# Contiguous gate and up halves in the weight slot, and expert rows fetched four experts ahead

## The reference

```python
scores = sigmoid(x @ router_w)
_, idx = top_k(scores + router_bias, 8)
wsel = sel / sum(sel) * 2.5                       # sel: the scores at idx
gates = sum(one_hot(idx, 64) * wsel[..., None], axis=1)
hid = silu(einsum('nd,edf->nef', x, exp_w_gate)) * einsum('nd,edf->nef', x, exp_w_up)
routed = einsum('nef,efd->nd', hid * gates[..., None], exp_w_down)
shared = (silu(x @ shared_w_gate) * (x @ shared_w_up)) @ shared_w_down
y = rmsnorm(x0 + g_f * (routed + shared))
```

## Time and profile before

| | us |
|---|---|
| three runs, median | 993.21 |
| lowest, highest | 984.48, 999.41 |
| profiled execution, first to last instruction (span) | 998.1 |
| TensorE busy in it | 798.7 (80%) |
| mean busy share of the 16 DMA engines, 350 to 955 us | 0.93 |

### The profile page before, as it was taken

The page is one execution under the profiler, slowest core; times in us unless marked ns, Lnnn a source line. Parts: engine busy times, 40 slices in busy tenths (PEclk is TensorE's granted clock), DMA queues, the critical chain, the costliest instruction groups (busy, mean ns, idle before and its releaser), DMA issues.

```text
span 998.1 us, 16529 instructions
## 1 busy us (share of the span) xinstructions
PE 798.7 (80%) x5564; PEld 449.7 (45%) x5565; DVE 393.9 (39%) x825; ACT 235.7 (24%) x405; POOL 306.1 (31%) x285
## 2 busy tenths in 40 slices
PE   1979999999888799876796888888788788887910
PEld 1657555445444355443443444444444344443500
DVE  2235183656144643233342343334334334444306
ACT  2112543023132222122121221222122122222202
POOL 0120000021133444344334343433334434344323
PEclk8879999999897889878888889887888988988965
DMA  9977846345689999989998999899899989999234
GB/s 273 398 244 240 304 164 231 117 149 212 226 251 362 367 318 334 324 251 348 311 316 287 315 316 327 252 349 310 281 340 321 360 285 334 358 331 353 68 58 145
DMA packets 192230, 277.75 MB, mean 278 GB/s; under 512 B 20355, under 2 KB 154931, under 8 KB 183548
## 3 DMA queue, kind: packets, MB, share of 16 engines
q1 hardware_dynamic: 165654, 250.88, 72.3%
q0 software_dynamic: 21216, 22.57, 10.2%
q10 hardware_dynamic: 5254, 2.76, 1.1%
HBM read 270.14 MB, written 25.89 MB: 297 GB/s over the span
## 4 chain that ended last, share of the span: by engine, by line
PE 54%; DMA 26%; issue 10%; DVE 6%; POOL 1%; POOLq 1%; ACT 1%; SPq 1%; DVEq 0%
DMA et<-xn_rows,idx 16%; PE bank L1049 15%; PE bank L1085 12%; DMA acc_rows<-et,idx 5%; PE bank L770 4%; PE bank L778 3%; PE bank L1032 3%; PE bank L913 3%; PE bank L797 2%; DMA gu<-in_ada_w 2%; PE bank L755 2%; DMA small<-halfc 2%; PE bank L1009 1%; PE bank L1136 1%; PE bank L781 1%
## 5 line engine op out<-in xcount | busy, mean ns | idle before, releaser
L1049 PE MATMUL bank<-gu,et 128*64 128x256 f32 x2496 | 295.9, 394 | 33.3 <-issue 31.0
L1049 PEld LDWEIGHTS bank<-gu,et 128*64 128x64 f32 x2496 | 185.6, 144 | 168.2 <-issue 91.4
L1085 PE MATMUL bank<-dn,et 128*64 128x512 f32 x624 | 183.5, 726 | 2.3 <-DVE et L1534 1.2
L449 POOL DMA_INDIRECT acc_rows<-et,idx x64 | 105.6, 1649 | 226.1 <-DVE et L1541 164.1
L430 POOL DMA_INDIRECT et<-xn_rows,idx x64 | 80.8, 1263 | 193.9 <-DVE idx L1516 133.7
L1534 DVE COPY et<-bank 128x256 f32<-128x256 f32 x64 | 27.1, 424 | 222.8 <-PE bank L1066 218.6
L690 ACT ACTIVATE et<-bank 64x512 f32<-64x512 f32 x64 | 37.8, 590 | 265.9 <-PE bank L1049 263.1
L1032 PE MATMUL bank<-ident,et 128*128 128x128 f32 x256 | 50.0, 328 | 62.3 <-DMA et<-xn_rows,idx 35.6
L1085 PEld LDWEIGHTS bank<-dn,et 128*64 128x64 f32 x624 | 46.6, 163 | 88.7 <-issue 88.7
L1520 DVE COPY et<-bank 128x512 f32<-128x512 f32 x64 | 44.3, 692 | 103.5 <-PE bank L1032 99.9
L1541 DVE TENSOR_SCALAR et<-bank,pick_out 128x512 f32<-128x512 f32 x64 | 48.1, 751 | 81.4 <-PE bank L1085 76.5
(11 more groups left out here) (269 smaller groups left out, 684.0 us busy)
## 6 DMA issues: line engine op xcount, KB each, us to landing
gu<-in_exp_w_gate SPq DMA_DIRECT2D x64, 1024.0 KB
gu<-in_exp_w_up SPq DMA_DIRECT2D x64, 1024.0 KB
dn<-in_exp_w_down SPq DMA_DIRECT2D x64, 1024.0 KB
gu<-in_ada_w SPq DMA_DIRECT2D x12, 2048.0 KB, 13.9
gu<-in_w_in SPq DMA_DIRECT2D x4, 2048.0 KB, 19.5
gu<-in_w_out SPq DMA_DIRECT2D x2, 2048.0 KB, 13.1
acc_rows<-dn SPq DMA_DIRECT2D x2, 1280.0 KB, 16.2
small<-halfc POOLq DMA_DIRECT2D x100, 0.0 KB
```

Source lines behind the costliest of these rows:

```text
L449: pool.indirect_dma_start(acc_rows[0], bass.IndirectOffsetOnAxis(ap=idx[:, u, 0:1], axis=0), yo[:, u % 2, 0, :], None, bounds_check=2 * T ...
L1049: mm = pe.matmul(bank[u % 2][64 * c:64 * c + 64, b * FE:(b + 1) * FE], xt[:, b, k % 4, k // 4, :], w[:, k, c * FE:(c + 1) * FE], start=(k ...
L1085: mm = pe.matmul(bank[5 + b][64 * c:64 * c + 64, :], hT[:, b, j, :], dn[:, dslot(u), j * D + c * HALF:j * D + (c + 1) * HALF], start=(j == ...
```

## The change

It does two things. First, a slot of `gu` is now seen as two halves of 8 KB per partition, [gate | up], so each gate and each up load (the shared expert's too) writes 8 KB in a row; the products read `w[:, c, k, :]` in place of `w[:, k, c*256:(c+1)*256]`. Second, G = 4: the gathers use four buffers (the two old ones, and the first two tiles of `xn`, which are free by then) and run four experts ahead, with four semaphores each for `gathered` and `gathered2`; select, pick and index move with them, from u+2 to u+4. Experts 2 and 3 are now picked and indexed before the loop.

```diff
+G = 4
+        xg_buf = [xg[:, 0], xg[:, 1]] + [xn[:, t, :].rearrange("p (s n) -> p s n", s=2) for t in range(2)]
...
-        eg = io["exp_w_gate"][0].rearrange("e (p k) f -> e p k f", k=KT)
+        eg = io["exp_w_gate"][0].rearrange("e (p k) f -> e p (k f)", k=KT)
...
+        def halves(slot):
+            return gu[slot][:, :, :].rearrange("p k n -> p (k n)").rearrange("p (c m) -> p c m", c=2)
+        def pair(slot):
+            return halves(slot).rearrange("p c (k f) -> p c k f", k=KT)
...
-                sync.dma_start(gu[gslot(u)][:, :, 0:FE], eg[e]).then_inc(ld_gu[gslot(u)], 16)
-                sync.dma_start(gu[gslot(u)][:, :, FE:2 * FE], eu[e]).then_inc(ld_gu[gslot(u)], 16)
+                sync.dma_start(halves(gslot(u))[:, 0, :], eg[e]).then_inc(ld_gu[gslot(u)], 16)
+                sync.dma_start(halves(gslot(u))[:, 1, :], eu[e]).then_inc(ld_gu[gslot(u)], 16)
...
+            pool.wait_ge(s["tp_ready"], TP["z11"] + 1)
...
-                if not (isinstance(e, int) and e < 2):
-                    pool.wait_ge(s["xt_ready"], e - 1)
+                if not (isinstance(e, int) and e < G):
+                    pool.wait_ge(s["xt_ready"], e - (G - 1))
...
-                    if not (last and u >= U - 2):
-                        gather(r, i + (u + 2) // U, (u + 2) % U)
+                    if not (last and u >= U - G):
+                        gather(r, i + (u + G) // U, (u + G) % U)
...
-                gather(r, 0, 0)
-                gather(r, 0, 1)
+                for u in range(G):
+                    gather(r, 0, u)
...
-                                           w[:, k, c * FE:(c + 1) * FE], start=(k == 0), stop=(k == KT - 1))
+                                           w[:, c, k, :], start=(k == 0), stop=(k == KT - 1))
...
-                    if not (last and u >= U - 2):
-                        pick(r, i + (u + 2) // U, (u + 2) % U)
+                    if not (last and u >= U - G):
+                        pick(r, i + (u + G) // U, (u + G) % U)
...
+                for u in range(2, G):
+                    pick(r, 0, u)
                 turn_x(r, 0, 0, is_full(r, 0, 0))
...
+                for u in range(2, G):
+                    select(r, 0, u)
+                    index(r, 0, u)
                 xt0(r, 0, 0)
```

More of the change, by code:

```diff
@@ L180, in build @@
         ld_shared_gu, ld_shared_dn = sem("ld_shared_gu"), sem("ld_shared_dn")
-        gathered = [sem("gathered0"), sem("gathered1")]
-        gathered2 = [sem("gathered2_0"), sem("gathered2_1")]
+        gathered = [sem(f"gathered{b}") for b in range(G)]
+        gathered2 = [sem(f"gathered2_{b}") for b in range(G)]
         scattered = [sem("scattered0"), sem("scattered1")]
@@ L190, in build @@
         wout_p = io["w_out"][0].rearrange("(k p) (j n) -> j p k n", p=P, n=512)
-        eg = io["exp_w_gate"][0].rearrange("e (p k) f -> e p k f", k=KT)
-        eu = io["exp_w_up"][0].rearrange("e (p k) f -> e p k f", k=KT)
+        eg = io["exp_w_gate"][0].rearrange("e (p k) f -> e p (k f)", k=KT)
+        eu = io["exp_w_up"][0].rearrange("e (p k) f -> e p (k f)", k=KT)
         ed = io["exp_w_down"][0].rearrange("e (p j) n -> e p (j n)", j=2)
@@ L296, in _ @@
             for c, name in enumerate(("shared_w_gate", "shared_w_up")):
-                sync.dma_start(gu[SH_SLOT][:, :, c * FE:(c + 1) * FE],
-                               io[name][0].rearrange("(p k) f -> p k f", k=KT)).then_inc(ld_shared_gu, 16)
+                sync.dma_start(halves(SH_SLOT)[:, c, :],
+                               io[name][0].rearrange("(p k) f -> p (k f)", k=KT)).then_inc(ld_shared_gu, 16)
             def load_gu(r, i, u):
@@ L426, in gather @@
                 pool.wait_ge(s["idx_ready"], e + 1)
-                if not (isinstance(e, int) and e < 2):
-                    pool.wait_ge(s["xt_ready"], e - 1)
+                if not (isinstance(e, int) and e < G):
+                    pool.wait_ge(s["xt_ready"], e - (G - 1))
                 pool.sem_inc(s["pool_go"], 1)
-                pool.indirect_dma_start(xg[:, u % 2, 0, :], None, xn_half,
+                pool.indirect_dma_start(xg_buf[u % G][:, 0, :], None, xn_half,
                                         bass.IndirectOffsetOnAxis(ap=idx[:, u, 0:1], axis=0),
-                                        bounds_check=2 * T - 1, oob_is_err=False).then_inc(gathered[u % 2], 16)
+                                        bounds_check=2 * T - 1, oob_is_err=False).then_inc(gathered[u % G], 16)
                 with pool.If(full):
-                    pool.indirect_dma_start(xg[:, u % 2, 1, :], None, xn_half,
+                    pool.indirect_dma_start(xg_buf[u % G][:, 1, :], None, xn_half,
                                             bass.IndirectOffsetOnAxis(ap=idx[:, u, 1:2], axis=0),
-                                            bounds_check=2 * T - 1, oob_is_err=False).then_inc(gathered2[u % 2], 16)
+                                            bounds_check=2 * T - 1, oob_is_err=False).then_inc(gathered2[u % G], 16)
                 with pool.Else():
-                    pool.dma_start(skipped[:, u:u + 1], halfc[0:1, :]).then_inc(gathered2[u % 2], 16)
+                    pool.dma_start(skipped[:, u:u + 1], halfc[0:1, :]).then_inc(gathered2[u % G], 16)
             def scatter(r, i, u):
@@ L945, in _, with shared_product @@
             wout(2, range(4, KT))
-            def shared_gu(t):
-                tile_product(bank[4 + t], t, gu[SH_SLOT], 2 * FE).then_inc(s["sh_ready"], 1)
+            def shared_product(t, ks):
+                t0, n = TILES[t]
+                w = pair(SH_SLOT)
+                for k in ks:
+                    if t < 2:
+                        mm = pe.matmul(bank[4 + t][:, :].rearrange("p (c f) -> p c f", c=2), xT[:, k, t0:t0 + n], w[:, :, k, :],
+                                       start=(k == 0), stop=(k == KT - 1))
+                    else:
+                        for c in range(2):
+                            mm = pe.matmul(bank[4 + t][64 * c:64 * c + 64, 0:FE], xT[:, k, t0:t0 + n], w[:, c, k, :],
+                                           start=(k == 0), stop=(k == KT - 1))
+                return mm
             def logits(t):
@@ L962, in _ @@
             pe.wait_ge(ld_shared_gu, 32)
-            tile_product(bank[4], 0, gu[SH_SLOT], 2 * FE, range(4))
+            shared_product(0, range(4))
             turn("z", "xn_ready", 1)
-            tile_product(bank[4], 0, gu[SH_SLOT], 2 * FE, range(4, KT)).then_inc(s["sh_ready"], 1)
+            shared_product(0, range(4, KT)).then_inc(s["sh_ready"], 1)
             pe.wait_ge(s["tp_evac"], TP["z11"] + 1)
@@ L981, in _ @@
             spread_gf(3)
-            tile_product(bank[5], 1, gu[SH_SLOT], 2 * FE, range(4))
+            shared_product(1, range(4))
             pe.wait_ge(s["mask_done"], 1)
@@ L995, in _ @@
             mm.then_inc(s["tp_ready"], 1)
-            tile_product(bank[5], 1, gu[SH_SLOT], 2 * FE, range(4, KT)).then_inc(s["sh_ready"], 1)
+            shared_product(1, range(4, KT)).then_inc(s["sh_ready"], 1)
             def pick(r, i, u):
@@ L1016, in turn_x @@
                 e = r * NE + i * U + u
-                pe.wait_ge(gathered[u % 2], 8 * (e - u % 2) + 16)
-                pe.wait_ge(gathered2[u % 2], 8 * (e - u % 2) + 16)
+                pe.wait_ge(gathered[u % G], (16 // G) * (e - u % G) + 16)
+                pe.wait_ge(gathered2[u % G], (16 // G) * (e - u % G) + 16)
                 if isinstance(e, int) and e == 0:
@@ L1027, in half @@
                     for k in range(4):
-                        pe.transpose(bank[2 + b][:, k * P:(k + 1) * P], xg[:, u % 2, b, k * P:(k + 1) * P], ident[:, :])
+                        pe.transpose(bank[2 + b][:, k * P:(k + 1) * P], xg_buf[u % G][:, b, k * P:(k + 1) * P], ident[:, :])
                 with pe.If(full):
@@ L1031, in turn_x @@
                 for k in range(4):
-                    mm = pe.transpose(bank[2][:, k * P:(k + 1) * P], xg[:, u % 2, 0, k * P:(k + 1) * P], ident[:, :])
+                    mm = pe.transpose(bank[2][:, k * P:(k + 1) * P], xg_buf[u % G][:, 0, k * P:(k + 1) * P], ident[:, :])
                 mm.then_inc(s["xt_ready"], 1)
@@ L1043, in gate_up @@
                     pe.wait_ge(s["up_evac"], e - 1)
-                w = gu[gslot(u)]
+                w = pair(gslot(u))
                 def blocks(b):
@@ L1152, in rounds @@
                     pe.wait_ge(s["gf_in"], 6)
-                    shared_gu(2)
+                    shared_product(2, range(KT)).then_inc(s["sh_ready"], 1)
                 pick(r, 0, 1)
@@ L1545, in body @@
                     before = (r, i if u else i - 1, (u - 1) % U)
-                    if not (last and u >= U - 2):
-                        select(r, i + (u + 2) // U, (u + 2) % U)
+                    if not (last and u >= U - G):
+                        select(r, i + (u + G) // U, (u + G) % U)
                     if not (first and u == 0):
                         ht(*before)
```

(4 more changed lines are left out.)

## The result

The changed kernel takes 932.4 us in the median (926.9 to 936.7, four runs) against 994.6 us (four runs too; the 993.21 of the table above is from three). The ratio is 0.940, with a 95% interval of 0.932 to 0.947, so it is 6% faster; 938 was forecast. The profiled execution has a span of 927.7 us.

A forecast was written before the change was run, and what follows sets the result against it. Gathers set TensorE's pace with DMA close behind; after the change the loads would bind. Span 998.1 - 56 (loop) + 2.5 - 2 = 942.6 us, and 4.9 lower for the median of runs: 938 us, range 900 to 978.

The forecast's parts named there:

- The gathers: Waits of TensorE at the turn for gathered rows: four buffers remove all 69.4 us, and 48 us of half-clock work.
- The loads: Gate and up loads in the expert loop: 8 KB rows save 0.75 us per expert, 39 us of DMA work.
- my 56: Time saved over the 56 experts of the loop: 549 us in place of 605, 56 us less.
- The sum under it: DMA work in the expert loop: 524 us in place of 563, plus 20 of tail and 5 of full slots, 549.
- rival B: Expert loop: loads gain nothing in mixed traffic, waits only change place, DMA work gives 588 us, time 976; chance 0.14.
- The scatters: Chain of scatters in the expert loop, the other bound: 10.4 us apart gives 582 us, 9.4 gives 526; 549 kept.
- Rival D: Scatters in the loop take turns with 8 KB weight rows: 2.1 us more each, time about 1088; chance 0.08.
- Before the loop: Ahead of the turn of expert 0: two selects, picks and indexes that nothing else hides, +2.5 us.
- The 2 us back in the first eight experts: First eight experts of the loop: gathers 2 and 3 go out at once, taking back waits of some 2 us.
- The loop passes: TensorE's waits ahead of gate_up, 31.0 us in 5 times: taken as the cost of new loop passes, left unchanged.
- What would show it: New profile: turn waits near zero, many short gate_up waits, about 335 GB/s, DMA share 0.97 or more, body 77 to 79 us.

The follow-up runs named there:

- e1: The changed kernel with look-ahead of four kept and weight rows put back to 1 KB pieces: 938.5 us, 0.940 of the kernel before.
- e4: The changed kernel with even and odd experts' scatters in two accumulators, and gate and up rows in 1 KB pieces: 936.5 us, 0.938 of the kernel before.
- e3: The changed kernel with scatters of even experts to one accumulator and of odd experts to the other: 888.8 us, 0.890 of the kernel before.
- e10: The changed kernel with gate, up and down rows all of 4 KB: 900.3 us, 0.902 of the kernel before.
- e5: The changed kernel with gate and up rows of 4 KB, one DMA per matrix: 915.5 us, 0.916 of the kernel before.
- e7: e3 with 16 experts in a loop body in place of 8: 889.4 us, 0.889 of the kernel before.
- e6: The changed kernel with each gate and up load made as two DMAs of 4 KB rows: 914.0 us, 0.913 of the kernel before.
- e12: The changed kernel with look-ahead of two and gate and up rows of 4 KB: 1004.1 us, 1.006 of the kernel before.
- e9: The changed kernel with gate and up rows of 2 KB, one DMA per matrix: 913.9 us, 0.914 of the kernel before.
- e2: The changed kernel with 8 KB rows kept and look-ahead of two: 1014.5 us, 1.013 of the kernel before.

## Why the prediction was right, and where it wasn't

The time, 938 against 932.4, lies inside the range, and the chain of reasons up to the gather holds. That the forecast came so close is in part luck: its sum went by the loads (9.8 us per expert), which don't bind the changed kernel, and the chain of scatters, which does, happens to need nearly the same (9.5 us).

- *The gathers.* I had all 69.4 us of waits at the turn go, and 48 us of half-clock work with them. 9.8 us are left, and the clock went from 0.88 to 0.94. The busy time fell by 28.6 us, not 48, in part at least since the new waits at the pick bring slow work back: after the one of 3.30 us that ends at 649.35, the turn took 1.11 us and the down product 2.99, as against 0.66 and 1.94 before it.
- *The loads.* This step failed: DMA work in the stretch falling by 39 us was most of my 56. On its own the look-ahead gives the whole gain (e1), and the 8 KB rows add nothing to it. The size of the term was about right for a kernel that the loads bind, 47.7 us between e4 and e3, but the changed kernel isn't one.
- *The sum under it.* I took 0.93 x 605 us of DMA share as work that can't shrink, which made 588 us the floor with 1 KB pieces and 976 us the time of rival B. e1 reaches 938.5 us with 1 KB pieces. A share counts the time in which packets are open, and two queues overlap to 1.05; the rate shows the room, 313 GB/s against the 350 of e1 and the 367 in short stretches. The waits would have told it too: before, TensorE waited for no expert's weights, and SP waited 390 us for free slots.
- *The scatters.* I named them as "the other bound", at 9.4 to 10.4 us, and went by the DMA sum of 9.8. They are the bound: spaced 9.48 us, at 9.55 us per expert, and with two accumulators the time falls to 888.8 us (e3). By this bound the answer would have come out of the right cause.
- *Rival D* had the right mechanism at a fraction of its price. I set it aside since gathers beside 1 KB pieces were no quicker in the trace of before; single latencies scatter by more than the effect. In steps of e10, e5 and the changed kernel the spacing grows from 9.00 over 9.25 to 9.48 us, some 0.25 us each, where I had priced 2.1 for the step from 1 to 8 KB. The rule I cited from the Trainium skill (DMA: Bandwidth & Descriptors, Queues, rings and completion order), that the engines change queue after a whole packet only, pointed the right way; no run here shows its packets.
- *Before the loop.* +2.5 us: the turn of expert 0 starts at 259.33 where it was 256.57, and the shared product ends 0.3 us sooner, so 3.1, close to the forecast. The 2 us back in the first eight experts are there too: the first scatter goes out at 290.52 where it was 287.71, and the eighth at 357.68 where it was 358.12.
- *The loop passes* I left at 31.0 us; they are 29.8 (five long waits, 28.5, and four short ones), and e7 confirms the cause.
- *What would show it.* GB/s in the loop 341 (335 forecast), with the tail without weights in it. The weights end near 860 us, and in 400 to 800 us the DMA share is 0.97, as I had said, at 365 GB/s. So the share met its mark though the loads don't bind; it was 0.96 in that window before. A body of eight took 77.2 us in the mean of four (77 to 79 forecast). The mark that told is gate_up, which got no new waits.

What stays open: why long rows hold the scatters up. That the engines take turns row by row fits e5, e6, e10 and e12, but not in a plain way e9, whose rows are half as long as those of e5 and whose scatters land no sooner; and no run looks at the turns themselves. In e3, the best here, TensorE is busy in 365 of 400 us, and 10.3 us are waits for weights; the shares of its chain by engine are

```profile
PE 76%; DMA 10%; DVE 6%; issue 5%; ACT 1%; SPq 1%; POOL 0%; POOLq 0%; DVEq 0%
```

So it goes mostly by TensorE's own work, with the loads close behind: in e7, with four of the five waits of the loop passes gone, DMAs take 31% of the chain, 24% the loads of the up matrix alone. No run shows what faster loads or less work on TensorE would bring from there.

## What to carry to other kernels

Look for the wait that stands next, and test a floor of the DMA engines by who waits for a load and by the rate, not by their busy share. Long rows make loads faster and small indirect transfers beside them slower, so their length is a matter of which of the two is on the path: 2 to 4 KB was best for gate and up while scatters were chained, and 8 KB no worse than 4 KB once they weren't. And a chain of accumulating scatters is cut in two by a second accumulator at no cost, if the end adds two of them anyway: this is worth 5% here with 8 KB rows (nothing with 1 KB pieces, where the loads bind), and e3 at 888.8 us (0.890) beats both kernels.

## What the runs showed that I had not expected

- A change of rows that gives 11% more rate in the loop where scatters are freed (e3 against e4: 388 and 350 GB/s) made the kernel of before 1.3% slower (e2).
- The best rows for the changed kernel are neither those of before nor the new ones: 2 KB and 4 KB rows give 914 and 915.5 us, 1 KB and 8 KB 938.5 and 932.4.
- DMA shares of 1.05 over 400 us, with two queues open; a share of 0.96 at 313 GB/s left room for 12% more rate with the same pieces (e1, 350).
